# Seven-product output projection: weight sums formed by GpSimd in attention steps 9 to 12, token-tile differences stored by the stages that make the tiles

## The chip, the cores and the metric

The kernel runs on one core of one Trainium2 chip. Five engines work side by side and meet only at semaphores: PE (TensorE, the matmuls), VectorE (DVE), ScalarE (ACT), GpSimd (POOL) and SyncE (SP), which here only issues DMAs. Each engine takes its instructions in program order, so an instruction that waits holds everything behind it on its engine. The metric is the device time of one execution in microseconds; the profile gives the span from the first to the last instruction of one execution.

## What is computed

One decoder layer with two parallel groups of heads, in float32. Cut to what matters:

```python
h    = rms_norm(x, pre_norm_w) * (1 + scale) + shift       # x: 2048 tokens x 1024
proj = h @ w_in                                            # GLA and SSD columns
o    = gla_chunked(q, k, v, log_a)                         # 4 heads, 1024 columns
o    = rms_norm(o, gla_norm_w) * silu(g)
y    = ssd_chunked(xs, dt, A, B, C) + d_skip * xs          # 2 groups, 1024 columns
y    = rms_norm(y * silu(z), ssd_norm_w)
mixed = concat(o, y) @ w_out                               # 2048 x 2048 @ 2048 x 1024
out  = x + gate * rms_norm(mixed, post_norm_w)
```

## The kernel before

Every large product is taken in three passes: a float32 value is split into a high part (ScalarE copies it to the rounded format) and a low part (VectorE subtracts the high part from the raw value), and PE adds high*high, high*low and low*high.

**front** (`front`) makes h and runs the GLA heads. It has 16 steps, `n`, four blocks of 512 tokens for each of four heads. A step has twelve slots `i` of some 3.5 us; in each PE does half a projection unit (`half_unit`) and one small piece of the attention of the step before: `scores` (L1066, L1069), `outputs` (L1079 to L1085) or `turn` (L1093), for tiles t = 0 to 3. For each tile ScalarE takes the mean square (L574), GpSimd turns it into 1/rms (`rstd_of`, L419 and L422), ScalarE scales (L578), PE transposes (L1093) and VectorE multiplies with the gate (`gated`, L808) into `y`. At slot 11 VectorE also makes the exponentials' products (`products`, L776 to L782), which PE needs in the first slot of the next step. SyncE's queue holds in each step the four loads of h for the step after the next (`load_h`, L302; each waits until VectorE has read the buffer, L737), in steps 3, 7, 11 and 15 also the six weight loads of the next head (`load_w`, L283; each waits for the `w_low`, L748, of two units before), and at the end `store_y` (L312), two DMAs that put `y` into the DRAM tensor `y_d` ("mixed_in"). The tile `late` (3 x 1024 columns) serves steps 5 to 7 and the end; between, it is free.

**ssd** (`ssd`) has 2 groups of 8 steps of 256 tokens. In a step PE does eight projection units (L1727, L1731) with the pieces of the step before between them. In the last step of all (15) SyncE loads the output weights of the first product (`load_w` with g = G, L1307): both halves of 512 columns, 512 KB each time, and VectorE subtracts one from the other (`w_minus`, L1572) before ScalarE and VectorE split the result (L1441, L1567). The first two units of the output projection run at the end of this stage (L1744).

**project_out** (`project_out`) multiplies 2048 x 2048 by 2048 x 1024 by Strassen's scheme: the tokens are taken as pairs of 128-token tiles, the columns in two halves, and `PRODUCTS` lists seven products, each of a sum of tiles and a sum of weight blocks. A unit `j` is one product for one pair of tiles (eight pairs, 56 units, 24 matmuls of 512 columns each, L2124). For unit `j` SyncE loads the tiles (`load_a`, L1918, L1920, L1923), GpSimd adds or subtracts them where the product has two terms (`a_sum`, L1980 to L1983), ScalarE takes the high part (`a_high`, L2022) and VectorE the low part (`a_low`, L2067), three units ahead on GpSimd and two on the others. Likewise for each of the 48 weight pieces of products 1 to 6: `load_w`, `w_sum` (32 of them), `w_high` (L2032), `w_low` (L2073). VectorE adds the results (`add`, L2087). A finished row of 128 tokens goes through ScalarE (`square`, L2046), GpSimd (`rstd_of`, L2000, L2003) and VectorE (`finish`, L2096, L2100) and is stored. During product 6 (j = 48 to 55) a row is finished per unit.

The order is written out by hand in the loops over `j`: on ScalarE a_high(j+2), w_high, copy(j), square; on VectorE a_low(j+2), the row of the unit before (`finish`), w_low, add(j); on GpSimd a_sum(j+3), w_sum, rstd.

```python
for j in range(IN_TAIL, N + 1):          # VectorE
    if j + 2 < N:
        a_low(j + 2)
    for m in range(len(rows)):
        if square_at[m] + 1 == j:
            finish(m)
```

## Time and profile before

| | us |
|---|---|
| three runs | 1753.59, 1759.62, 1761.76; median 1759.62 |
| the profiled execution | 1755.11, its span 1753.3 |
| PE busy | 1641.5 (94%) |
| VectorE busy | 1025.4 (58%) |
| ScalarE busy | 843.3 (48%) |
| GpSimd busy | 401.0 (23%) |
| front, by the last PE work before the gap | about 0 to 792 |
| ssd | about 797 to 1416 |
| project_out | 1421.1 to 1753.3 |

PE's figure is time in which a matmul was open, not its peak. Its granted clock has two levels, 1.0 (2.4 GHz) and 0.5 (1.2 GHz), and was 0.975 in the mean of the span. The page's strip of 40 slices shows PE at eight or nine tenths from the third slice to the last but one, and VectorE rising from four tenths in front over seven in ssd to nine at the end. So a time is read from PE's gaps: where they are, what ended them, and at what clock PE worked after them.

### The profile page before, as it was taken

The page shows a single profiled execution, that of the slowest core. Times are in us where ns is not written, and L with a number is a line of the kernel's source. Part 1 is how long each engine was busy: PE and PEld are TensorE (multiplying, and loading weights), DVE is VectorE, ACT ScalarE, POOL GpSimd, SP SyncE. Part 2 cuts the span into 40 slices and gives each one's busy share as a digit, 9 for nine tenths or more (in the row PEclk, how much of TensorE's full clock was granted, in tenths as well). Part 3 has the DMA queues.
Part 4 walks back from the last instruction along what each step waited for, and adds up shares of the span by engine and source line. Part 5 has one row for each costly group of instructions (what it writes and reads, how often), then busy time and mean ns, then how long its engine had stood idle before and what let it go on. Part 6 is the DMA issues. An engine that isn't in the chain of part 4 may idle for free. (4 is left out here: it accounts for less than half of the span.)

```text
span 1753.3 us, 27317 instructions
## 1 busy us (share of the span) xinstructions
PE 1641.5 (94%) x10022; PEld 1409.5 (80%) x10022; DVE 1025.4 (58%) x1744; ACT 843.3 (48%) x1496; POOL 401.0 (23%) x441
## 2 busy tenths in 40 slices
PE   5799899999999999988999998999999889999985
PEld 5688788887888888878888887888888768888864
DVE  4443444453444443355677767777766746866986
ACT  5555455545544554464445555544554533334222
POOL 5000000010000001000222221222222237762652
PEclk9999999999999999998999999999999899999997
DMA  9422152235212421224212125212223357876785
GB/s 285 147 91 98 49 170 71 67 109 166 63 61 70 135 73 61 84 61 132 67 64 68 67 91 161 86 67 67 72 79 100 109 197 262 290 260 229 295 291 167
DMA packets 126622, 222.75 MB, mean 127 GB/s; under 512 B 9267, under 2 KB 77123, under 8 KB 122422
## 3 DMA queue, kind: packets, MB, share of 16 engines
q1 hardware_dynamic: 121302, 203.34, 36.0%
q10 hardware_dynamic: 4384, 17.83, 2.8%
q0 software_dynamic: 832, 0.22, 0.2%
q8 instruction: 62, 1.02, 0.2%
q14 instruction: 42, 0.34, 0.1%
HBM read 187.54 MB, written 33.82 MB: 126 GB/s over the span
## 5 line engine op out<-in xcount | busy, mean ns | idle before, releaser
L1042 PE MATMUL ps<-hl,w 128*128 128x512 f32 x1488 | 374.7, 401 | 0.1
L1042 PEld LDWEIGHTS ps<-hl,w 128*128 128x128 f32 x1488 | 275.8, 189 | 57.2 <-issue 1.4
L1727 PE MATMUL ps<-hl,w 128*128 128x256 f32 x2304 | 295.7, 289 | 4.7 <-PEq L266 4.7
L1727 PEld LDWEIGHTS ps<-hl,w 128*128 128x128 f32 x2304 | 283.6, 194 | 13.1 <-issue 13.1
L1048 PE MATMUL ps<-w,hl 128*128 128x256 f32 x1536 | 204.6, 291 | 2.0 <-DVE w L748 2.0
L1048 PEld LDWEIGHTS ps<-w,hl 128*128 128x128 f32 x1536 | 194.6, 195 | 4.9 <-DVE w L748 2.4
L2124 PE MATMUL ps<-w,hl 128*128 128x512 f32 x720 | 173.6, 403 | 14.0 <-DVE hl L2067 5.3
L1731 PE MATMUL ps<-hl 128*128 128x512 f32 x768 | 178.6, 391 | 0.0
L1600 DVE SCALAR_TENSOR_TENSOR c_acc<-c_before,conv_col,c_acc 128x256 f32<-128x256 f32 x288 | 142.0, 493 | 62.1 <-ACT c_acc L1462 55.1
L2124 PEld LDWEIGHTS ps<-w,hl 128*128 128x128 f32 x720 | 139.9, 196 | 47.1 <-DVE hl L2067 7.5
L1731 PEld LDWEIGHTS ps<-hl 128*128 128x128 f32 x768 | 143.0, 188 | 29.3
L419 POOL TENSOR_SCALAR mse<-ms 128x1 f32<-128x1 f32 x60 | 15.8, 263 | 636.6 <-ACT squares L574 636.6
L1460 ACT ACTIVATE c_before<-ps 128x256 f32<-128x256 f32 x96 | 36.9, 384 | 216.0 <-PE ps L1727 216.0
L2124 PE MATMUL ps<-hl 128*128 128x512 f32 x576 | 131.8, 390 | 2.6 <-DVE hl L2067 2.6
L2124 PEld LDWEIGHTS ps<-hl 128*128 128x128 f32 x576 | 108.0, 188 | 25.9 <-DVE hl L2067 3.5
L798 DVE SCALAR_TENSOR_TENSOR state<-state,dec,ps 128x256 f32<-128x256 f32 x56 | 26.9, 480 | 134.7 <-PE ps L1085 134.7
L737 DVE TENSOR_TENSOR hl<-x_sb,hl 128x1024 fp32r<-128x1024 f32 x48 | 58.7, 1222 | 57.5 <-ACT hl L558 57.5
L1399 POOL TENSOR_TENSOR c_yi<-c_yi,c_xd 128x512 f32<-128x512 f32 x32 | 41.3, 1291 | 186.5 <-DVE c_yi L1640 186.5
L1384 POOL TENSOR_TENSOR c_xend<-c_xdt,tok 128x512 f32<-128x512 f32 x32 | 33.5, 1046 | 215.6 <-DVE c_xdt L1620 215.6
L2067 DVE TENSOR_TENSOR hl<-d_a_raw,hl 128x1024 fp32r<-128x1024 f32 x35 | 63.6, 1818 | 25.7 <-ACT hl L2022 25.6
L748 DVE TENSOR_TENSOR w<-w_raw,w 128x1024 fp32r<-128x1024 f32 x30 | 36.5, 1223 | 59.3 <-ACT w L504 59.3
L808 DVE SCALAR_TENSOR_TENSOR y<-ps,norm_col,gz 128x128 f32<-128x128 f32 x120 | 36.3, 344 | 55.2 <-PE ps L1093 43.2
(251 smaller groups left out, 2648.5 us busy)
## 6 DMA issues: line engine op xcount, KB each, us to landing
x_sb<-h SPq DMA_DIRECT2D x52, 512.0 KB, 3.9
d_a_raw<-mixed_in SPq DMA_DIRECT2D x22, 1024.0 KB, 7.2
w_raw<-in_w_in SPq DMA_DIRECT2D x42, 512.0 KB, 4.5
c_ac<-step_sums ACTq DMA_DIRECT2D x16, 1024.0 KB, 4.7
w_raw<-in_w_out SPq DMA_DIRECT2D x32, 512.0 KB, 4.9
c_h_raw<-h SPq DMA_DIRECT2D x56, 256.0 KB, 2.8
late_w<-mixed_in SPq DMA_DIRECT2D x10, 1024.0 KB, 7.3
d_a_raw<-mixed_in SPq DMA_DIRECT2D x18, 512.0 KB, 4.7
```

What stands on the lines that cost most here:

```text
L737: last = dve.tensor_tensor(hl[:, n % 2, ks, LO, :], raw, hl[:, n % 2, ks, HI, :].bitcast(F32), ALU.subtract)
L748: dve.tensor_tensor(lo, w_raw[:, u % 2], hi.bitcast(F32), ALU.subtract).then_inc(w_ready, 1)
L808: last = dve.scalar_tensor_tensor(out=y[:, t, f, :], in0=ps[:, TURNS, f * P:(f + 1) * P], scalar=norm_col[:, f:f + 1], in1=gz[:, r % 2, f, ...
L1042: mm = pe.matmul(ps[:, PROJ + u % 2, :], w[:, u, k, a, :], hl[:, par, k, b, :], start=(k == 0 and i == 0), stop=(k == KT - 1 and i == 2))
L1048: mm = pe.matmul(ps[:, PROJ + u % 2, half * DV:(half + 1) * DV], hl[:, par, k, a, t * P:(t + 1) * P], w_v[:, k, b, :], start=(k == 0 and i ...
L1399: pool.tensor_tensor(yi[:, :, :], yi[:, :, :], xd[:, :, :], ALU.add).then_inc(skip_ready, 1)
L1460: act.activation(before[:, u, HIST:], ps[:, PROJ + u % 2, 0:B2], ACT.Copy)
L1600: op = dve.scalar_tensor_tensor(out=acc[:, u, :], in0=before[:, u, k:k + B2], scalar=conv_col[:, k, ch:ch + 1], in1=acc[:, u, :], op0=ALU. ...
L1727: mm = pe.matmul(ps[:, PROJ + u % 2, 0:B2], w[:, u, k, a, :], hl[:, par, k, b, :], start=(k == 0 and i == 0), stop=(k == KT - 1 and i == 2))
L1731: mm = pe.matmul(ps[:, PROJ + u % 2, :], hl[:, par, k, a, t * P:(t + 1) * P], w_z[:, k, b, :], start=(k == 0 and i == 0), stop=(k == KT - ...
L2067: dve.tensor_tensor(half[:, :, LO, :], a_term(j, 0).rearrange("p (f n) -> p f n", n=P), half[:, :, HI, :].bitcast(F32), ALU.subtract).then ...
L2124: mm = pe.matmul(ps[:, j % 8, :], halves[:, j % 4, k, a, :], weight(i)[:, k, b, :], start=(k == 0 and q == 0), stop=(k == KT - 1 and q == 2))
```

## The change

It does four things.

1. **Sums of weights in front.** In steps 9 to 12 SyncE loads, for each of the eight row blocks f of `w_out`, the four 128 x 512 quarters (1 MB, `load_quarters`) into `late`, GpSimd makes five sums (`out_sum`: 4 = 1-3, 5 = 0+1, 1 = 0+3, 3 = 2+3, 2 = 2-0) and SyncE stores the five (1280 KB, `store_sums`) into the DRAM tensor `w_sum_d`. Two blocks are done in a step. The next block is loaded only when the stores of the block before have landed (`small_stored`).
2. **Differences of tiles.** After each step of front VectorE makes `y_diff`, tile 1 minus tile 0 of each pair (128 x 512), and SyncE stores it as a third tile of `y_d`; in ssd GpSimd does it (`c_y_diff`, 128 x 512). `y`'s buffer is free again when all three stores have landed.
3. **ssd's last step** loads the ready difference of the weights (256 KB) and drops `w_minus`.
4. **project_out** loads every weight piece as one piece of 256 KB; `w_sum` is gone (32 instructions). Products 1 and 6 take the stored tile difference as one term: 16 of the 40 `a_sum` are gone, 24 are left. Products, rows and order are otherwise as they were.

Besides, `squares` is written in bfloat16 and some small tiles share memory.

```diff
@@ front, SyncE
                 def put_y(n):
                     h, s = n // NB, n % NB
                     for b in range(B1 // B2):
-                        sp.dma_start(y_d[s * (B1 // B2) + b, :, :, h * 2:h * 2 + 2, :],
+                        sp.dma_start(y_d[s * (B1 // B2) + b, :, 0:2, h * 2:h * 2 + 2, :],
                                      y[:, 2 * b:2 * b + 2, :, :]).then_inc(y_stored, 16)
+                    sp.wait_ge(diff_ready, n + 1)
+                    sp.dma_start(y_d[s * (B1 // B2):(s + 1) * (B1 // B2), :, 2, h * 2:h * 2 + 2, :]
+                                 .rearrange("b p f n -> p b f n"), y_diff[:, :, :, :]).then_inc(y_stored, 16)
+
+                def load_quarters(f):
+                    sp.wait_ge(small_stored, 32 + f * 16)
+                    sp.dma_start(quarters[:, 0:4, :].rearrange("p (s c) n -> p s (c n)", s=2), out_rows[f]
+                                 ).then_inc(rows_loaded, 16)
+
+                def store_sums(f):
+                    sp.wait_ge(out_summed, 5 * f + 5)
+                    sp.dma_start(w_sum_d[f], quarters[:, 1:6, :]).then_inc(small_stored, 16)
...
                     for q in range(KT // 2):
+                        if q == 2 and SUMS_AT <= n < SUMS_AT + KT // 2:
+                            store_sums(2 * (n - SUMS_AT))
+                            load_quarters(2 * (n - SUMS_AT) + 1)
                         if NB <= n + 2 <= STEPS:
                             load_h(n + 2, q)
...
                     if n > 0:
                         store_y(n - 1)
+                    if SUMS_AT <= n < SUMS_AT + KT // 2:
+                        store_sums(2 * (n - SUMS_AT) + 1)
+                    if SUMS_AT - 1 <= n < SUMS_AT + KT // 2 - 1:
+                        load_quarters(2 * (n - SUMS_AT) + 2)
@@ front, GpSimd
+                def out_sum(f, i):
+                    if i == 0:
+                        pool.wait_ge(rows_loaded, 32 + 16 * f + 16)
+                    to, a, b, op = ((4, 1, 3, ALU.subtract), (5, 0, 1, ALU.add), (1, 0, 3, ALU.add), (3, 2, 3, ALU.add),
+                                    (2, 2, 0, ALU.subtract))[i]
...
+                    pool.tensor_tensor(quarters[:, to, :], quarters[:, a, :], quarters[:, b, :], op).then_inc(out_summed, 1)
...
                 for n in range(STEPS):
                     if n > 0:
                         rstd_of((n - 1) * TB)
+                    if SUMS_AT <= n < SUMS_AT + KT // 2:
+                        for i in range(3):
+                            out_sum(2 * (n - SUMS_AT), i)
...
                     if n > 0:
                         for t in range(1, TB):
                             rstd_of((n - 1) * TB + t)
+                            if SUMS_AT <= n < SUMS_AT + KT // 2:
+                                for i in ((3, 4), (0, 1, 2), (3, 4))[t - 1]:
+                                    out_sum(2 * (n - SUMS_AT) + t // 2, i)
@@ front, VectorE
                     last.then_inc(y_ready, 1)
+                    if t == TB - 1:
+                        difference(r * TB + TB)
+
+                def difference(done):
+                    dve.wait_ge(y_ready, done)
+                    dve.tensor_tensor(y_diff[:, :, :, :], y[:, 1::2], y[:, 0::2], ALU.subtract).then_inc(diff_ready, 1)
@@ ssd, SyncE (store_y), GpSimd, VectorE
+                    sp.wait_ge(diff_ready, r + 1)
+                    sp.dma_start(y_d[bass.ds(b, 1), :, TB2, f:f + XT, :].rearrange("a p f n -> (a p) f n"),
+                                 y_diff[:, :, :]).then_inc(y_stored, 16)
...
                     for t in range(TB2):
                         rstd_of(r, t)
+                    pool.wait_ge(y_ready, r * TB2 + TB2)
+                    wait(pool, y_stored, r * 32)
+                    pool.tensor_tensor(y_diff[:, :, :], y[:, 0], y[:, 1], ALU.subtract).then_inc(diff_ready, 1)
...
-                        if last_of_group and g + 1 == G and u > 0:
-                            if u > 1:
-                                w_low(G, u - 2)
-                            w_minus(u - 1)
@@ project_out
-    (((0, 0, -1), (1, 0, 1)), ((0, 0, 1), (0, 1, 1)), (((1, 1), 1),)),
+    (((2, 0, 1),), ((0, 0, 1), (0, 1, 1)), (((1, 1), 1),)),
...
-    (((0, 1, 1), (1, 1, -1)), ((1, 0, 1), (1, 1, 1)), (((0, 0), 1),)),
+    (((2, 1, 1),), ((1, 0, 1), (1, 1, 1)), (((0, 0), 1),)),
 )
+W_SUMS = (3, 4, 0, None, 1, None, 2)
...
-                    for v in W_AT.get(j, ()):
-                        w_sum(v)
```

**SyncE's queue around step 11 of front.** The first listing is of before, the second of the change; L numbers are each file's own, a row is one kind of instruction with its count. `w_raw<-in_w_in` is a weight load, `x_sb<-h` a load of h, `w_sums<-late` a `store_sums`, `late<-in_w_out` a `load_quarters`.

```order
58 L283 DMA w_raw<-in_w_in 128x8x128 x2
59 L302 DMA x_sb<-h 128x1024
60 L283 DMA w_raw<-in_w_in 128x8x128
61 L302 DMA x_sb<-h 128x1024
62 L283 DMA w_raw<-in_w_in 128x8x128 x2
63 L302 DMA x_sb<-h 128x1024
64 L283 DMA w_raw<-in_w_in 128x8x128
```

```order
77 L330 DMA w_sums<-late 128x2560
78 L325 DMA late<-in_w_out 128x2x1024
79 L288 DMA w_raw<-in_w_in 128x8x128 x2
80 L307 DMA x_sb<-h 128x1024
81 L288 DMA w_raw<-in_w_in 128x8x128
82 L307 DMA x_sb<-h 128x1024
83 L288 DMA w_raw<-in_w_in 128x8x128 x2
84 L330 DMA w_sums<-late 128x2560
85 L325 DMA late<-in_w_out 128x2x1024
86 L307 DMA x_sb<-h 128x1024
87 L288 DMA w_raw<-in_w_in 128x8x128
```

One store and one load of sums stand ahead of the head's first weight load, and another pair stands in the middle of the step, behind the fourth and fifth weight loads.

**GpSimd in steps 9 to 12.** Before, it holds only the pairs `mse`, `rstd`, one for each tile; here are two and a half such pairs, and then the change in step 9.

```order
101 L419 TENSOR_SCALAR mse<-ms 128x1
102 L422 TENSOR_TENSOR rstd<-mse,neg_half 128x1
103 L419 TENSOR_SCALAR mse<-ms 128x1
104 L422 TENSOR_TENSOR rstd<-mse,neg_half 128x1
105 L419 TENSOR_SCALAR mse<-ms 128x1
```

```order
106 L445 TENSOR_TENSOR rstd<-mse,neg_half 128x1
107 L456 TENSOR_TENSOR late<-late 128x512 x3
108 L442 TENSOR_SCALAR mse<-ms 128x1
109 L445 TENSOR_TENSOR rstd<-mse,neg_half 128x1
110 L456 TENSOR_TENSOR late<-late 128x512 x2
111 L442 TENSOR_SCALAR mse<-ms 128x1
112 L445 TENSOR_TENSOR rstd<-mse,neg_half 128x1
113 L456 TENSOR_TENSOR late<-late 128x512 x3
114 L442 TENSOR_SCALAR mse<-ms 128x1
115 L445 TENSOR_TENSOR rstd<-mse,neg_half 128x1
116 L456 TENSOR_TENSOR late<-late 128x512 x2
```

Three sums now stand between the 1/rms of tiles 0 and 1 and between those of tiles 2 and 3, two behind those of tiles 1 and 3.

**VectorE in ssd's last step.** `c_acc` is the convolution, `w_raw<-w_raw` is `w_minus`, `c_yi` begins `tile_out`.

```order
1104 L1600 SCALAR_TENSOR_TENSOR c_acc<-c_before,conv_col,c_acc 128x256 x3
1105 L1572 TENSOR_TENSOR w_raw<-w_raw 128x512
1106 L1600 SCALAR_TENSOR_TENSOR c_acc<-c_before,conv_col,c_acc 128x256 x3
1107 L1580 TENSOR_TENSOR hl<-c_h_raw,hl 128x4x128
1108 L1567 TENSOR_TENSOR w<-w_raw,w 128x512
1109 L1572 TENSOR_TENSOR w_raw<-w_raw 128x512
1110 L1640 TENSOR_TENSOR c_yi<-ps,tok 128x512
```

```order
1120 L1647 SCALAR_TENSOR_TENSOR c_acc<-c_before,conv_col,c_acc 128x256 x6
1121 L1619 TENSOR_TENSOR w<-w_raw,w 128x512
1122 L1627 TENSOR_TENSOR hl<-c_h_raw,hl 128x4x128
1123 L1687 TENSOR_TENSOR c_yi<-ps,tok 128x512
```

Both `w_minus` ahead of `c_yi` are gone, and the one split that is left stands behind the second convolution.

## Rows read from the trace of the kernel before

**Rows 1.** Waits of PE: who, for what, us in total, times, longest.

```profile
PE ps L2124 <- DVE hl L2067: 7.9, 5, 2.9
...
PE ps L1772 <- DVE c_btok L1629: 7.3, 3, 3.7
...
PE ps L1066 <- DVE y L808: 9.7, 7, 2.3
...
PE ps L1066 <- DVE dec L782: 4.5, 10, 0.5
```

**Rows 2.** Stretches of L2124: us, PE busy (matmuls), clock, DMA share, GB/s.

```profile
1421.10:1657.20 236.10, 235.49 (x1026) 0.99 0.79 272
...
1657.20:1737.70 80.50, 69.09 (x271) 0.92 0.75 249
```

**Rows 3.** PE in order of time: start, us, line [idle before <-releaser].

```profile
1456.07 43.74 PE L2124 MATMUL ps<-hl 128*128 128x512 f32 x192
```

**Rows 4.** All engines after an idle stretch: the clock is third from the end.

```profile
1421.00:1425.00 4.00, 3.86 (x9) 3.12 (x10) 0.00 (x0) 1.08 (x2) 0.13 (x2) 0.50 0.68 181
```

**Rows 5.** VectorE in order of time, inside the last product.

```profile
1693.32 0.68 DVE L2087 TENSOR_TENSOR d_mixed<-d_mixed,ps 128x512 f32<-128x512 f32 x1
...
1696.16 3.41 DVE L2067 TENSOR_TENSOR hl<-d_a_raw,hl 128x1024 fp32r<-128x1024 f32 x1 [2.17 <-ACT hl L2022]
...
1701.95 0.68 DVE L2087 TENSOR_TENSOR d_mixed<-d_mixed,ps 128x512 f32<-128x512 f32 x1
...
1730.65 1.23 DVE L2067 TENSOR_TENSOR hl<-d_a_raw,hl 128x1024 fp32r<-128x1024 f32 x1 [2.17 <-ACT hl L2022]
...
1744.88 0.68 DVE L2087 TENSOR_TENSOR d_mixed<-d_mixed,ps 128x512 f32<-128x512 f32 x1
```

**Rows 6.** GpSimd in order of time, same row of output.

```profile
1696.11 2.39 POOL L1982 TENSOR_TENSOR d_a_raw<-d_a_raw 128x1024 f32<-128x1024 f32 x1
```

**Rows 7.** PE in order of time, SSD steps 15 and 8.

```profile
1107.01 1.15 PE L1772 MATMUL ps<-c_xdt,c_decay 128*64 128x64 f32 x32
...
1108.66 6.31 PE L1727 MATMUL ps<-hl,w 128*128 128x256 f32 x48
...
1368.37 1.97 PE L1772 MATMUL ps<-c_xdt,c_decay 128*64 128x64 f32 x32 [3.32 <-DVE c_btok L1629]
...
1371.36 7.80 PE L1727 MATMUL ps<-hl,w 128*128 128x256 f32 x48
```

**Rows 8.** VectorE in order of time, SSD step 15.

```profile
1358.30 0.69 DVE L1572 TENSOR_TENSOR w_raw<-w_raw 128x512 f32<-128x512 f32 x1 [4.07 <-DMA w_raw<-in_w_out]
...
1368.03 0.28 DVE L1629 COPY c_btok<-ps 128x128 f32<-128x128 f32 x1
```

**Rows 9.** SyncE's queue in order of time, end of step 10 and step 11.

```profile
570.05 1.20 SPq L312 DMA_DIRECT2D mixed_in<-y  x2
...
591.52 11.06 SPq L283 DMA_DIRECT2D w_raw<-in_w_in  x2
```

**Rows 10.** DMA issues: out<-in, engine, count, KB each, median us to landing.

```profile
c_ac<-step_sums ACTq DMA_DIRECT2D x16, 1024.0 KB, 4.7
...
mixed_in<-c_y SPq DMA_DIRECT2D x16, 512.0 KB, 3.0
```

**Rows 11.** One microsecond of a store: DMA share and GB/s stand last.

```profile
1015.00:1016.00 1.00, 1.00 (x11) 1.00 (x10) 0.93 (x3) 0.00 (x0) 0.00 (x0) 1.00 1.03 403
```

**Rows 12.** GpSimd's addition of two 128x512 tiles: busy, mean ns, idle before.

```profile
L1399 POOL TENSOR_TENSOR c_yi<-c_yi,c_xd 128x512 f32<-128x512 f32 x32 | 41.3, 1291 | 186.5 <-DVE c_yi L1640 186.5
```

**Rows 13.** PE in order of time, step 11: second and last transposition.

```profile
587.10 0.38 PE L1093 MATMUL ps<-ident,o_n 128*128 128x128 f32 x2
...
608.39 0.38 PE L1093 MATMUL ps<-ident,o_n 128*128 128x128 f32 x2
```

**Rows 14.** VectorE in order of time, end of step 11.

```profile
608.21 1.23 DVE L737 TENSOR_TENSOR hl<-x_sb,hl 128x1024 fp32r<-128x1024 f32 x1 [2.01 <-ACT hl L558]
```

**Rows 15.** ScalarE in order of time, SSD step 7.

```profile
1056.03 1.06 ACT L1437 ACTIVATE w<-w_raw 128x1024 fp32r<-128x1024 f32 x1 [4.71 <-DMA w_raw<-in_w_in]
```

136 lines of the change are left out of this document (60 added, 76 removed).

## The prediction

> **What bounds the kernel now.** I read the list of waits first, then each engine in order of time at the places that the change touches, then the DMA issues. PE is open 94% of the span, so only its gaps and the clock behind them can be won or lost. The list of PE's waits shows 7.9 us in the projection for VectorE's low parts, 7.3 us in ssd for `c_btok` (3.7 the longest), 9.7 us in front for `y`, and ten very short waits for the exponentials' products (`dec`, at most 0.5 us) [rows 1]. Those ten cost nothing, but they say that VectorE has no room at the end of a step of front. The table by stretch shows the projection's matmuls back to back at clock 0.99 up to 1657.2; from there to 1737.7, where PE ends, 271 of them took 80.50 us [rows 2]. Undisturbed, 192 take 43.74 us, so 0.228 each and 5.47 for a unit of 24 [rows 3]. The 271 would be 61.8 us: 18.7 us are lost in the last product and the end of the one before it, in gaps and in matmuls at half clock behind them. A gap costs more than itself: the four microseconds from 1421, right behind the empty stretch between ssd and the projection, ran at 0.50 [rows 4], and the 9 matmuls in them are 2.1 us at full clock. So I put 1.9 to 2.8 us on top of a gap of several us and nothing on one under 1 us.
>
> The sum is made against the profiled execution, 1755.11 us, which lies 4.5 us (0.3%) under the median of the three runs, 1759.62. I forecast the difference and take it from the median.
>
> **Gain 1, the projection's last product.** Why it is slow stands on VectorE. `a_low` takes 3.41 us at 1696.16 and 1.23 us at 1730.65, same shape and form [rows 5]. The difference is GpSimd: its `a_sum` began at 1696.11 and held 2.39 us [rows 6]; the last unit has none beside it. So the two exclude each other, and the later one waits 2.18. From addition to addition, VectorE's round for a unit is 1701.95 - 1693.32 = 8.6 us [rows 5] against PE's 5.47: VectorE is the bound. The changed kernel takes the stored difference in product 6, so no `a_sum` stands beside these eight units: 8.6 - 2.2 = 6.45 a round. This is still over 5.47; VectorE stays the bound, only less. Undisturbed PE would end at 1657.2 + 61.8 = 1719, and unit 48, seven units earlier, at 1681. From there five rounds of 6.45 and two of some 5.3 (the last have no `a_low`) end near 1724, where the last addition was at 1744.88 [rows 5]: 21 us, and at most 22. VectorE comes out of product 5 behind, though, since `a_sum` remains there and its rounds have little to spare beside PE's. I take **19.5**, range 14 to 22.
>
> The Trainium skill, page "SBUF — State Buffer", section "Who interferes with whom", says: VectorE and GpSimd share a pair of ports under an exclusive lock, a VectorE instruction with two SBUF inputs needs it, and whoever starts first holds it for the whole instruction. By that rule the trace agrees, 3.41 against 1.23; it also speaks against the front half of this change (cost 3).
>
> **Gain 2, ssd's step 15.** VectorE waits 4.07 us there for 512 KB of `w_out` and then subtracts; `c_btok`, behind it in order, comes at 1368.03 [rows 8], and PE stood 3.32 us for it, from 1365.05 [rows 7]. The unit behind this stop took 7.80 us where the same unit in step 8 took 6.31; from the start of the L1772 matmuls to that unit's end it is 10.79 us in step 15 and 7.96 in step 8 [rows 7], so 2.8 are the clock. With both `w_minus` and this wait gone (4.07 + 0.69 for the one shown) `c_btok` comes before PE asks. 3.3 + 2.8, nearly: **6**, range 2 to 7 (another load behind it may be late next).
>
> **Cost 1, the second pair in step 11.** SyncE's queue is in order, and step 11 loads the next head's weights, each when a `w_low` has freed its buffer. Two were issued in the 11.06 us from 591.52, the second at 602.6 [rows 9]. The change puts `store_sums` and `load_quarters` of the odd block behind them. Store issued at about 602.4; 3.0 us for the first 512 KB [rows 10] and 1.95 for the other 768 KB at 403 GB/s [rows 11], with some queueing 5.2 (up to 6). Then the load of 1 MB, 4.7 by the row of the same size [rows 10], 4.9 beside other traffic, and the two weight loads in front of it some 1.2 more. The quarters are there at about 613.8. GpSimd holds three sums ahead of the 1/rms of tile 3: 3 x 1.29 by its addition of the same size [rows 12] = 3.9; the two small instructions of the 1/rms 0.9 and ScalarE's scaling 0.5, both my estimates: 619.1. PE transposes tile 3 at 608.39 today [rows 13]. Stall **10.7** (9 to 14), and **2.5** of half clock behind it [rows 4]. Nothing covers it: everything on PE stands behind this transposition.
>
> **Cost 2, the first pair at step boundaries.** Let T0 be 21.0 us ahead of tile 1's transposition, 566.1 for the one at 587.10 [rows 13]; it is the step's start on PE. `store_y` is issued at 570.05 [rows 9], T0 + 3.9. Behind it now come VectorE's difference and its store, then `store_sums` at T0 + 5.7, with the `y` transfers still in flight: landed T0 + 11.7, quarters T0 + 16.7, three sums to T0 + 20.6, 1/rms and scaling to T0 + 22.0. So 1.0 in each of steps 10 and 11, **2.0** together (0 with a quick round trip; 6 with half clock). Steps 9 and 12 have slack: in 9 the load is issued a step early, 12 begins behind the stall. The odd blocks of steps 9, 10 and 12 meet no weight load: sums by T0 + 39, the 1/rms of tile 3 at T0 + 39.7; no stall, with 0.7 to spare.
>
> **Cost 3, sums beside VectorE at the end of a step.** The last two sums of a step stand behind the 1/rms of tile 3, and VectorE then takes the low part of h, two SBUF inputs, 1.23 at 608.21 [rows 14], and behind it the products for which PE waits already [rows 1]. One sum ahead of it delays it by up to 1.29 [rows 12]. Three boundaries (steps 9, 10, 12; in 11 it drowns in the stall) x 1.2 = **3.6**, range 0 to 4. By the skill's rule it is nothing where VectorE starts first; the sum would then be 3.6 lower.
>
> **Small ones.** The difference of 128x512 (0.69, as `w_minus` [rows 8]) stands ahead of low parts that PE waits for in steps 1 and 2, and the third store delays `y`'s release once: **2.3** (0 to 4). In the other steps it hides in the time in which `y` waits for ScalarE and GpSimd. At the ends of front and ssd a difference and a 256 KB store (under the 3.0 of 512 KB [rows 10]) stand behind the last `y`, partly beside the stores of before: **1.3** (0 to 4). In ssd's step 7 the weight load waits behind `diff_ready` on SyncE, and ScalarE already waits 4.71 for it [rows 15], PE 3.7 behind that [rows 1]: **1.5** (0 to 3). GpSimd's other differences in ssd lie in its idle time, 186 us before one line alone [rows 12]. `w_sum` gone from the projection gives nothing up to 1657, since nothing is lost there [rows 2].
>
> **Sum.** Gains 19.5 + 6 = 25.5. Costs 10.7 + 2.5 + 2.0 + 3.6 + 2.3 + 1.3 + 1.5 = 23.9. Net -1.6: 1753.5 on the profile's scale, **1758.0** on the median's. A measurement of this kernel tells about 0.5% from no change, 8.8 us: 1750.8 to 1768.4 is the same.
>
> **Rivals.**
> (A) *The round trip is quick.* Store and load take 8 us instead of 10.1, VectorE starts first at the boundaries, and the projection gains its full 22. For it: doubling a transfer from 512 KB to 1 MB added only 1.7 us [rows 10]. Cost 1 falls by 2.1, cost 2 by 2.0, cost 3 by 3.6, gain 1 rises by 2.2, the small ones fall by 1: -1.6 - 10.9 = -12.5, so 1747.
> (B) *Slower: the round trip takes 13 us.* Its place is the wait for the landed stores ahead of every `load_quarters`. For it: the store is larger than any in the trace, and loads of h and `y` share the queue. Tile 1 in steps 10 and 11 then stalls 4.1 instead of 1.0 (+6.2, and +5 of half clock), step 11's second pair costs 3.1 more, the odd blocks of 9, 10 and 12 some 0.8 each: +16.8, so -1.6 + 16.8 = +15.2: 1775. It decides from about 12 us on. Against it: 4.7 for 1 MB [rows 10].
> (C) *The projection gains 10 only*, because VectorE leaves product 5 more than a unit behind, with up to 2.4 of exclusion for each `a_sum` [rows 6]: +9.5, 1767.5. Against it: up to 1657.2 PE lost nothing [rows 2].
>
> The same skill's page "DMA: Bandwidth & Descriptors", section "Anatomy of one DMA — SWDGE (gpsimd) path", puts about 2 us fixed on each transfer of GpSimd's queue. These transfers are SyncE's, and no run here shows whether it carries over; by it store and load would be 5.0 + 4.4 = 9.4 us, cost 1 0.7 lower.
>
> **Chances.** My forecast 0.42, (A) 0.30, (B) 0.19, (C) 0.09, half of which falls to either side of the bound. Faster by over 0.5%: 0.30; within: 0.46; slower: 0.24. The range, 1743 to 1776, takes in most of (A) and (B); what lies outside is a round trip under 7 or over 13 us.
>
> **What would show it.** Right: one gap of some 11 us in step 11 ahead of the last transposition, released by ScalarE behind GpSimd's sums behind the quarters; `a_low` at 1.23 throughout product 6 and its round at 6.45; no gap at `c_btok` in step 15, a longer one in step 7. Wrong: gaps of more than 2 us at tile 1 in steps 10 and 11, or at tile 3 in steps 9, 10, 12 (B); an `a_low` of 3 us in product 6, or additions late at its start (C); a store and load well under 10 us from issue to landing (A). The forecast fails altogether if the loss in the last 100 us has another cause than VectorE's round: then PE's gaps there stay.

## The result

| | before | changed | ratio |
|---|---|---|---|
| median of 11 runs, us | 1757.92 | 1771.04 | 1.0064, 95% interval 1.0048 to 1.0081 |
| lowest and highest, us | 1753.59, 1764.65 | 1766.75, 1775.01 | |
| span of the profiled execution, us | 1753.3 | 1767.4 | |

The changed kernel is slower, by 0.64%, some 11 to 14 us. The forecast was 1.6 us faster. The two spans differ by 14.1 us, and it can be split at the two places where PE waits for its sequencer, the starts of ssd (796.72 before, 838.84 after) and of the projection (1421.14 and 1457.70):

| stage | before, us | changed, us | difference | forecast |
|---|---|---|---|---|
| front | 796.7 | 838.8 | +42.1 | +21.6 |
| ssd | 624.4 | 618.9 | -5.6 | -3.7 |
| projection | 332.2 | 309.7 | -22.5 | -19.5 |
| sum | 1753.3 | 1767.4 | +14.1 | -1.6 |

The forecast column shares the prediction's 1.3 us for the ends of the stages out as 0.5 for front and 0.8 for ssd. So two stages came out as forecast or better, and front cost twice what it was to cost.

The waits of PE in the changed kernel (who, for what; us in total, times, longest) answer to [rows 1]. The projection's wait for `hl` is gone; a new wait of 24 us for `o_n`, ScalarE's scaled tile, stands first:

```profile
PE ps L1140 <- ACT o_n L618: 24.0, 8, 11.9
```

**The projection.** Two stretches of PE's matmuls there, as in [rows 2]: us, PE busy (matmuls), clock, DMA share, GB/s. There is no gap left; the 8.6 us rounds of [rows 5] are 1728.93 - 1722.49 = 6.44 us, and `a_low` takes 1.23 throughout:

```profile
1457.70:1710.00 252.30, 252.29 (x1103) 0.99 0.69 232
1710.00:1754.10 44.10, 44.07 (x195) 1.00 0.67 209
```

```profile
1718.89 1.23 DVE L2086 TENSOR_TENSOR hl<-d_a_raw,hl 128x1024 fp32r<-128x1024 f32 x1 [2.17 <-ACT hl L2044]
...
1722.49 0.68 DVE L2106 TENSOR_TENSOR d_mixed<-d_mixed,ps 128x512 f32<-128x512 f32 x1
...
1728.93 0.68 DVE L2106 TENSOR_TENSOR d_mixed<-d_mixed,ps 128x512 f32<-128x512 f32 x1
```

**Front, tile by tile.** The changed kernel's transposition of a tile, less the same one before, is 6.9 us at the start of step 9 and 41.7 us at the start of step 13; it is 41.8 in step 15 too. All of the loss beyond the first 6.9 us lies in the four steps that form sums. PE in order of time there (start, us, line, count, [idle before <- who ended it]), the counterparts of [rows 13]: the last transpositions of steps 9, 10 and 11, the second of step 11, and the first matmul of step 11:

```profile
534.12 0.64 PE L1140 MATMUL ps<-ident,o_n 128*128 128x128 f32 x2 [2.90 <-ACT o_n L618]
...
581.15 0.44 PE L1140 MATMUL ps<-ident,o_n 128*128 128x128 f32 x2 [1.71 <-ACT o_n L618]
...
586.82 0.33 PE L1113 MATMUL ps<-ident,k_end 128*128 128x128 f32 x1 [2.47 <-DVE dec L822]
...
606.95 0.44 PE L1140 MATMUL ps<-ident,o_n 128*128 128x128 f32 x2 [2.42 <-ACT o_n L618]
...
641.89 0.69 PE L1140 MATMUL ps<-ident,o_n 128*128 128x128 f32 x2 [11.93 <-ACT o_n L618]
```

The forecast had the 11.93 us (as 10.7) and stops at tile 1 of steps 10 and 11 (1.0 each; 1.08 and 2.42 came). It had nothing at tile 3 of steps 9, 10 and 12 (2.90, 1.71 and 1.91) and nothing at tile 1 of step 12 (1.80).

What GpSimd does at these places: it waits for the quarters (`late<-in_w_out`), forms three sums, and only then makes the 1/rms that ScalarE and PE wait for:

```profile
528.72 3.89 POOL L456 TENSOR_TENSOR late<-late 128x512 f32<-128x512 f32 x3 [9.75 <-DMA late<-in_w_out]
532.69 0.22 POOL L442 TENSOR_SCALAR mse<-ms 128x1 f32<-128x1 f32 x1
...
636.54 3.82 POOL L456 TENSOR_TENSOR late<-late 128x512 f32<-128x512 f32 x3 [19.47 <-DMA late<-in_w_out]
```

And SyncE's queue: `store_sums`, then `load_quarters`, which waits for the landing of the store, so the distance between the two issues is the store's time. The rows at the end of step 10 and in step 11 answer to [rows 9]:

```profile
515.30 0.43 SPq L330 DMA_DIRECT2D w_sums<-late  x1
523.73 0.38 SPq L325 DMA_DIRECT2D late<-in_w_out  x1
...
541.77 0.50 SPq L330 DMA_DIRECT2D w_sums<-late  x1
547.77 0.38 SPq L325 DMA_DIRECT2D late<-in_w_out  x1
...
614.22 9.76 SPq L288 DMA_DIRECT2D w_raw<-in_w_in  x2
624.03 0.58 SPq L330 DMA_DIRECT2D w_sums<-late  x1
631.02 0.37 SPq L325 DMA_DIRECT2D late<-in_w_out  x1
```

The store of 1280 KB took 8.4 us right behind a load of h (515.30 to 523.73), 6.0 behind `y` (541.77 to 547.77) and 7.0 behind two weight loads (624.03 to 631.02); the load then took 5.0 (528.72 - 523.73), 5.1 and 5.5. Over all seven pairs the store took 7.3 to 8.4 us where a load of h stands right in front, 6.0 to 6.8 behind `y`, and store and load together took 10.9 to 13.4 us. The forecast put 10.1 for the two alone, 11.0 behind `y` (cost 2) and 11.4 behind the weight loads (cost 1); rival (B) put 13.

### The profile page after: what moved, and what is told of

Its sections match the earlier page's. It is cut to its first block and busy times, and to the rows that moved or that the text cites. A ratio compares the mean times of both kernels' runs of the same rounds, so it can differ in the third digit from the quotient of the medians.

```text
span 1767.4 us, 27409 instructions
## 1 busy us (share of the span) xinstructions
PE 1637.2 (93%) x10022; PEld 1407.8 (80%) x10022; DVE 1044.2 (59%) x1752; ACT 842.1 (48%) x1496; POOL 387.2 (22%) x449
## 5 line engine op out<-in xcount | busy, mean ns | idle before, releaser
L1089 PE MATMUL ps<-hl,w 128*128 128x512 f32 x1488 | 380.4, 405 | 0.1
L1647 DVE SCALAR_TENSOR_TENSOR c_acc<-c_before,conv_col,c_acc 128x256 f32<-128x256 f32 x288 | 161.9, 563 | 47.0 <-ACT c_acc L1514 40.1
L2143 PE MATMUL ps<-w,hl 128*128 128x512 f32 x720 | 166.3, 393 | 5.1 <-PEq L1347 5.1
L2143 PEld LDWEIGHTS ps<-hl 128*128 128x128 f32 x576 | 108.1, 188 | 22.5
L777 DVE TENSOR_TENSOR hl<-x_sb,hl 128x1024 fp32r<-128x1024 f32 x48 | 63.2, 1317 | 80.8 <-ACT hl L598 80.8
L618 ACT ACTIVATE o_n<-ps,rstd 128x256 f32<-128x256 f32 x60 | 28.5, 475 | 96.6 <-POOL rstd L445 96.6
L456 POOL TENSOR_TENSOR late<-late 128x512 f32<-128x512 f32 x40 | 54.0, 1360 | 73.8 <-DMA late<-in_w_out 72.6
```

Source lines behind the costliest of these rows:

```text
L456: pool.tensor_tensor(quarters[:, to, :], quarters[:, a, :], quarters[:, b, :], op).then_inc(out_summed, 1)
L777: last = dve.tensor_tensor(hl[:, n % 2, ks, LO, :], raw, hl[:, n % 2, ks, HI, :].bitcast(F32), ALU.subtract)
L1089: mm = pe.matmul(ps[:, PROJ + u % 2, :], w[:, u, k, a, :], hl[:, par, k, b, :], start=(k == 0 and i == 0), stop=(k == KT - 1 and i == 2))
L1647: op = dve.scalar_tensor_tensor(out=acc[:, u, :], in0=before[:, u, k:k + B2], scalar=conv_col[:, k, ch:ch + 1], in1=acc[:, u, :], op0=ALU. ...
L2143: mm = pe.matmul(ps[:, j % 8, :], halves[:, j % 4, k, a, :], weight(i)[:, k, b, :], start=(k == 0 and q == 0), stop=(k == KT - 1 and q == 2))
```

## The experiments

All ratios are against the kernel before, run on the same chip. "Distance" is the start of a PE transposition in the profile of a kernel less the start of the same one in the kernel before.

### What the sums cost in all

```diff
@@ e1_no_sums, from the changed kernel
-                            store_sums(...); load_quarters(...)      # all of them
-                                    out_sum(...)                     # all of them
-                        src = w_sum_d[f, :, W_SUMS[i], :]
+                        src = w_rows[f, :, 0, 0:HN]
```

> The changed kernel without the loads, sums and stores of w_out in front; ssd and the projection read plain quarters of w_out in the places of the sums, with the same bytes and instructions (so the product is another one). Theory 1 (the 35 us that front loses in steps 9 to 12 all hang on the sums): 1771 - 35 = 1736 us, ratio to before 0.988. Theory 2 (a good part of it is the tile differences on VectorE and SyncE): 1745 to 1755. The 6.9 us lost before step 9 stay under both.

Measured: 1732.3 us, ratio 0.9868 (0.9847 to 0.9889). The steps 9 to 12 of front lose nothing (the distance to before is 1.7 us at the start of step 9 and 1.8 in step 15), ssd is 618.5 and the projection 309.9 us long as in the changed kernel. So the sums cost 35 us in steps 9 to 12; theory 1. The other 4 to 5 us of the difference lie ahead of step 9, where this profile has lost 1.7 us and not the 6.9 that both theories had left in place.

### Is it step 11, the length of the round trip, or the sums themselves?

```diff
@@ e2_skip11, from the changed kernel: SyncE and GpSimd
+    SUM_STEPS = (9, 10, 12, 13)
-                        if q == 2 and SUMS_AT <= n < SUMS_AT + KT // 2:
+                        if q == 2 and n in SUM_STEPS:
```

> The sums in steps 9, 10, 12 and 13; step 11, which loads the next head's weights, has none. All eight blocks are made, nothing else is moved. Theory 1a (step 11's 12 us stall is the weight loads on SyncE's queue in front of the odd block's store): step 11 costs nothing, step 13 costs what step 12 does (4 to 6 us): 18 - 5 = 13 us less, 1758. Theory R (the sums themselves, which shut VectorE out of its ports, cost the time wherever they are): 1768 to 1771.

Measured: 1753.7 us, ratio 0.9979 (0.9963 to 0.9995), 17.3 us under the changed kernel. In step 11 nothing is lost. Tile 3 of steps 9, 10 and 12 and tile 1 of step 10 keep their stops, and step 13 has stops of its own. The two rows are tile 3 of steps 9 and 12:

```profile
532.59 0.53 PE L1141 MATMUL ps<-ident,o_n 128*128 128x128 f32 x2 [2.73 <-ACT o_n L619]
...
667.95 0.44 PE L1141 MATMUL ps<-ident,o_n 128*128 128x128 f32 x2 [2.27 <-ACT o_n L619]
```

In the changed kernel steps 11 and 12 grow by 18.4 and 6.1 us; here steps 12 and 13, with the same four blocks, grow by 4.5 and 6.5. So theory 1a is shown: the weight loads in front of the store are worth 13 to 14 us of the 35. The other 21 are in the steps with sums wherever these stand.

```diff
@@ e4_short_store, from the changed kernel
-                    sp.dma_start(w_sum_d[f], quarters[:, 1:6, :]).then_inc(small_stored, 16)
+                    sp.dma_start(w_sum_d[f, :, 0:1], quarters[:, 1:2, :]).then_inc(small_stored, 16)
```

> The changed kernel, but of the five sums of a block only one is stored (256 KB instead of 1280 KB) and every reader reads that one; loads, sums and their order stay. Theory 1 (length of the round trip): the store takes 3 to 3.5 us instead of 6 to 8, so the round trip 8.5 instead of 12.5; the stalls at tile 3 in steps 9, 10 and 12 and at tile 1 in steps 10, 11 and 12 go, that of step 11's tile 3 falls from 11.9 to 8: 14 to 16 us less, 1756. Theory R: 1770, nothing changes.

Measured: 1751.8 us, ratio 0.9966 (0.9944 to 0.9987), 19 us less. With 256 KB the store takes 2.9 us behind `y` (536.35 to 539.28), and 4.7 behind a load of h:

```profile
513.24 0.43 SPq L330 DMA_DIRECT2D w_sums<-late  x1
517.95 0.38 SPq L325 DMA_DIRECT2D late<-in_w_out  x1
...
536.35 0.51 SPq L330 DMA_DIRECT2D w_sums<-late  x1
539.28 0.38 SPq L325 DMA_DIRECT2D late<-in_w_out  x1
```

The stops at tile 1 and at tile 3 of steps 9 and 10 are gone and that of tile 3 of step 12 is 0.3 us; 9.4 us are left in step 11 (11.9 with the long store). All 40 sums are still there. What this run leaves standing is a second, smaller thing that the long stops had covered: at the steps' boundaries PE waits 2.2 us (2.5 at the last) for `dec` instead of 0.4. Two things make up these 1.8 us. GpSimd's last two sums run from 528.08 to 530.74, and VectorE's low part of h, 1.23 us in [rows 14], takes 2.22 beside the second of them: 1.0. It also starts 0.8 us later against PE's transposition than in the kernel before, because ScalarE makes the high part of h behind the scaling of tile 3, and that stands behind the late 1/rms:

```profile
528.08 2.66 POOL L456 TENSOR_TENSOR late<-late 128x512 f32<-128x512 f32 x2
```

```profile
529.60 2.22 DVE L777 TENSOR_TENSOR hl<-x_sb,hl 128x1024 fp32r<-128x1024 f32 x1 [2.77 <-ACT hl L598]
```

```profile
534.36 0.33 PE L1113 MATMUL ps<-ident,k_end 128*128 128x128 f32 x1 [2.20 <-DVE dec L822]
```

By the rule of the Trainium skill weighed in the prediction (page "SBUF — State Buffer", section "Who interferes with whom") this would be nothing if VectorE starts first. It did not: GpSimd started 1.5 us earlier and its second sum, begun at about 529.4, was under way when VectorE started at 529.60, so the trace agrees with the rule, and here it is GpSimd that starts first.

### The same sums where their quarters have landed

```diff
@@ e3_spread, from e2_skip11: GpSimd and SyncE
                         rstd_of((n - 1) * TB)
+                    if n in SUM_STEPS:
+                        for i in range(5):
+                            out_sum(2 * SUM_STEPS.index(n), i)
...
                             rstd_of((n - 1) * TB + t)
+                            if n in SUM_STEPS and t == 2:
+                                for i in range(5):
+                                    out_sum(2 * SUM_STEPS.index(n) + 1, i)
...
+                        if q == 1 and n in SUM_STEPS:
+                            store_sums(2 * SUM_STEPS.index(n))
+                            load_quarters(2 * SUM_STEPS.index(n) + 1)
+                        if q == 3 and n in SUM_STEPS:
+                            store_sums(2 * SUM_STEPS.index(n) + 1)
+                            load_quarters(2 * SUM_STEPS.index(n) + 2)      # but the last
```

> As the run before, and each block's five sums stand together where its quarters have landed already: behind the 1/rms of tile 0 and of tile 2; its store and the next load stand on SyncE between the loads of h. Theory 1 (PE stalls because GpSimd holds the 1/rms behind sums that wait for a round trip of 12 to 13 us): no stall above 1 us is left in steps 9 to 13, front loses the 7 us before step 9 and 1 to 3 more: 1771 - 33 = 1738, ratio 0.989. Theory R (port exclusion of the 40 sums, 54 us on GpSimd): at least half of the 35 us stays, over 1752.

Measured: 1730.2 us, ratio 0.9852 (0.9835 to 0.9868): 41 us under the changed kernel, 28 under the one before, with the same 40 sums, the same eight stores and loads and the same bytes. The distance to the kernel before is 4.0 us at the start of step 9 and 4.1 at the start of step 14, behind the last step with sums. GpSimd's five sums are 7.62 us in one piece and start without a wait, at once behind the 1/rms of tile 0; the work for tile 1 is due 9.4 us after their start:

```profile
494.74 0.22 POOL L445 TENSOR_SCALAR mse<-ms 128x1 f32<-128x1 f32 x1 [9.65 <-ACT squares L617]
...
495.58 7.62 POOL L459 TENSOR_TENSOR late<-late 128x512 f32<-128x512 f32 x5
505.01 0.22 POOL L445 TENSOR_SCALAR mse<-ms 128x1 f32<-128x1 f32 x1 [1.82 <-ACT squares L617]
```

```profile
503.22 0.34 SPq L331 DMA_DIRECT2D w_sums<-late  x1
507.91 0.38 SPq L326 DMA_DIRECT2D late<-in_w_out  x1
...
523.72 0.33 SPq L331 DMA_DIRECT2D w_sums<-late  x1
529.98 0.38 SPq L326 DMA_DIRECT2D late<-in_w_out  x1
```

The store takes 4.7 us where it is issued 2.5 us behind a load of h (503.22 to 507.91) and 6.3 where it is issued 1.2 us behind one (523.72 to 529.98). Theory 1 is shown; the exclusion between the 40 sums and VectorE costs PE nothing in steps 9, 10, 12 and 13, where VectorE has slack. The time is 8 us under the expected 1738, since the steps with sums lose nothing and the first eight lost 4.0 us in this profile, not 7.

```diff
@@ e5_spread_with_11, from e3_spread
-    SUM_STEPS = (9, 10, 12, 13)
+    SUM_STEPS = (9, 10, 11, 12)
```

> e3_spread, but with the sums in steps 9, 10, 11 and 12 as in the changed kernel: only the order on GpSimd and SyncE differs from it. Theory 1 (GpSimd's order decides): in step 11 the second block's store waits for the weight loads, its load lands some 12 us into step 12, and the sums of that step, which stand behind the 1/rms of tile 0, end before tile 1 needs its own: at most 2 us are lost, 1730 to 1733. Rival 1a (the weight loads on SyncE's queue cost by themselves, whatever the order): 8 to 12 us of step 11's stall are back, 1740 or more.

Measured: 1737.5 us, ratio 0.9886 (0.9863 to 0.9909). In the profile the steps 9 to 12 lose 3.6 us, between the two theories and near the first. They stand at three places: ahead of tile 3's `outputs` in step 11, at the first slot of step 12, and ahead of tile 1's `outputs` in step 12:

```profile
613.28 0.28 DVE L831 COPY_PREDICATED att<-causal,ps 128x128 f32<-128x128 int32 x1
613.67 0.67 PE L1129 MATMUL ps<-v,att 128*128 128x256 f32 x2 [0.95 <-issue]
...
622.93 0.33 PE L1116 MATMUL ps<-ident,k_end 128*128 128x128 f32 x1 [1.51 <-DVE dec L825]
...
635.05 0.61 DVE L851 SCALAR_TENSOR_TENSOR y<-ps,norm_col,gz 128x128 f32<-128x128 f32 x2 [3.74 <-DMA mixed_in<-y_diff]
...
637.86 0.67 PE L1129 MATMUL ps<-v,att 128*128 128x256 f32 x2 [1.28 <-issue]
```

The profile names nothing for the first and the last ("issue"), but `outputs` waits for `att`, and VectorE's copy of `att` ends just before PE goes on (613.28 + 0.28, and 637.47 + 0.29). It is late in step 11 because the low part of h ahead of it takes 1.80 us beside the five sums, and in step 12 because VectorE first waits 3.74 us for the store of `y_diff`, which now lies behind a store and a load of sums in the queue, and then takes 1.97 us for the low part of h beside the next sums. The 1.51 us come from the 1/rms of tile 3: it stands behind five sums that took 9.40 us here, and ScalarE's high part of h stands behind it. So in this order too the sums cost something around the step in which VectorE also splits the next head's weights.

The rest of the 7 us to e3_spread lies ahead of step 9, where the two kernels are the same. So it was run again:

> e5_spread_with_11 once more. Its profile was 4.9 us later than e3_spread at the start of step 9 although the two are the same up to there. Scatter of one execution: this time the first eight steps lie 1 to 5 us behind the kernel before and the time is 1733 to 1738. A property of the program: 8 to 9 us again.

Measured: 1737.1 us, ratio 0.9863 (0.9840 to 0.9886), and 5.6 us at the start of step 9 instead of 8.9; steps 9 to 12 lose 4.1. So the 8.9 was scatter in part: the distance is 0.6 above the expected 1 to 5, and the time is in the expected range. Here the copy of `att` in step 11 is later still: PE stops 1.85 us for it at 611.24, and the four microseconds from 611 have a granted clock of 0.60. Of the 7 us to e3_spread's median some 4 are these two steps; why the other 3 stay is open.

### Where the projection's gain comes from

```diff
@@ e7_before_no_a6, from the kernel before: PRODUCTS, product 6
-    (((0, 1, 1), (1, 1, -1)), ((1, 0, 1), (1, 1, 1)), (((0, 0), 1),)),
+    (((0, 1, 1),), ((1, 0, 1), (1, 1, 1)), (((0, 0), 1),)),
```

> The kernel before with one term less in product 6: its tiles are loaded and taken alone, so the eight a_sum of the last product are left out (the result of that product is another one). Theory D: rounds of 6.45 instead of 8.6, 1758 - 18 = 1740, ratio 0.990. Theory W: w_sum is still there and VectorE comes late out of product 5: gain of 10 at most, 1748.

Measured: 1741.0 us, ratio 0.9910 (0.9886 to 0.9933), 17 us less. That is theory D. The projection is 316.8 us long, 15.4 less than before; `a_low` is 1.8 us in the first two units of product 6 and 1.2 in the other six, and the round from addition to addition is 1699.62 - 1693.18 = 6.44:

```profile
1696.03 1.22 DVE L2067 TENSOR_TENSOR hl<-d_a_raw,hl 128x1024 fp32r<-128x1024 f32 x1 [2.17 <-ACT hl L2022]
```

```diff
@@ e6_sums_only, from e3_spread: no y_diff anywhere, PRODUCTS 1 and 6 as before
-    (((2, 1, 1),), ((1, 0, 1), (1, 1, 1)), (((0, 0), 1),)),
+    (((0, 1, 1), (1, 1, -1)), ((1, 0, 1), (1, 1, 1)), (((0, 0), 1),)),
```

> e3_spread without any difference of tiles: products 1 and 6 form theirs by a_sum on GpSimd as the kernel before does, all else as in e3_spread. Theory D (the projection's gain is product 6 without a_sum): 21 us of the gain are lost and 4 us of front and 1 of ssd come back: 1730 + 16 = 1746. Theory W (the 32 w_sum that are gone carry half of the projection's gain): 1735.

Measured: 1738.6 us, ratio 0.9903 (0.9871 to 0.9936), between the two theories. Its projection is 326.1 us long, 6.1 less than before, without any difference of tiles: the missing `w_sum`, with weight loads of half the size, are worth that; the two were not taken apart. 15.4 + 6.1 = 21.5 is nearly the 22.5 of both together. In product 6 its VectorE stands as in [rows 5], and PE's waits for `hl` are back, 2.82 us the longest:

```profile
1680.38 3.41 DVE L2073 TENSOR_TENSOR hl<-d_a_raw,hl 128x1024 fp32r<-128x1024 f32 x1 [2.17 <-ACT hl L2031]
```

This run also prices the differences in ssd: its ssd is 615.1 us long, 9.3 less than before, where e3_spread has 618.7. So `w_minus` and its wait were worth 9.3, and the stored differences cost 3.6 of it.

### Are the differences worth their price?

```diff
@@ e8_ssd_diffs, from e3_spread: front makes and stores no difference
-    (((2, 0, 1),), ((0, 0, 1), (0, 1, 1)), (((1, 1), 1),)),
+    (((0, 0, -1), (1, 0, 1)), ((0, 0, 1), (0, 1, 1)), (((1, 1), 1),)),
```

> e3_spread without the differences in front: they serve product 1 alone, where PE loses nothing; product 1 goes back to a_sum, product 6 keeps the differences that ssd makes. Theory F (front's differences cost 2 to 5 us of late y and give nothing): 1726 to 1728, ratio 0.983. Rival (product 1's a_sum shuts VectorE out and PE waits there, or the 4 us are scatter of the first steps): 1730 to 1736.

Measured: 1727.0 us, ratio 0.9826 (0.9807 to 0.9846). The projection is as long as in e3_spread (308.8 and 308.6), so product 1's differences gave nothing. Run again:

> e8_ssd_diffs once more, beside the run before on the same chip: 1727; its first eight steps of front within 2 us of the first time.

Measured: 1728.2, ratio 0.9823 (0.9807 to 0.9838). The distance to before at the start of step 9 is 1.5 and 0.3 us in these two, -0.2 in e6_sums_only, 2.7 and 1.4 in the two runs below: 1.1 in the mean of the five. In the seven profiles whose front makes differences ahead of step 9 (the changed kernel, e1 to e5 and e5_again) it is 6.9, 1.7, 5.5, 4.0, 4.8, 8.9 and 5.6, in the mean 5.3. So they cost some 4 us. Most of it stands in step 7: from its first to its last transposition all seven lose 3.0 to 4.7 us, and the five without differences between -0.7 and 2.3. In the changed kernel VectorE waits 8.74 us for the third store before it can write `y` (5.66 us for the stores of `y` in the kernel before), and PE stops 4.05 us behind it (0.97 before):

```profile
413.02 0.61 DVE L848 SCALAR_TENSOR_TENSOR y<-ps,norm_col,gz 128x128 f32<-128x128 f32 x2 [8.74 <-DMA mixed_in<-y_diff]
```

The intervals of e3_spread and e8_ssd_diffs overlap; that the difference of 2 to 3 us is real rests on these anchors, not on the times.

```diff
@@ e9_diff_later, from e8_ssd_diffs: GpSimd in ssd
-                    for t in range(TB2):
-                        rstd_of(r, t)
-                    pool.wait_ge(y_ready, r * TB2 + TB2)
-                    wait(pool, y_stored, r * 32)
-                    pool.tensor_tensor(y_diff[:, :, :], y[:, 0], y[:, 1], ALU.subtract).then_inc(diff_ready, 1)
+                    rstd_of(r, 0)
+                    if not (isinstance(r, int) and r == 0):
+                        difference(r - 1)      # waits for y_stored >= r * 32 + 16 of its own r
+                    rstd_of(r, 1)
```

> e8_ssd_diffs with GpSimd's difference of ssd moved: it stands between the 1/rms of the two tiles of the next step, where GpSimd is idle, and its store one step later on SyncE. Theory P (the 3.9 us that the differences cost in ssd come from VectorE being shut out: its three convolution instructions take 3.02 us beside GpSimd's difference and 1.53 without): ssd 615 to 616 us long instead of 619, 1724 in all. Rival S (they come from the second store on SyncE and its wait): 1727, ssd unchanged.

What it rests on: VectorE's three convolution instructions (`c_acc` x3) in step 8 of ssd, in e8_ssd_diffs, what GpSimd does there, and then the same three in e6_sums_only:

```profile
1096.73 3.02 DVE L1640 SCALAR_TENSOR_TENSOR c_acc<-c_before,conv_col,c_acc 128x256 f32<-128x256 f32 x3 [1.47 <-ACT c_acc L1507]
```

```profile
1095.46 1.30 POOL L1463 TENSOR_TENSOR c_y_diff<-c_y 128x512 f32<-128x512 f32 x1 [10.46 <-ACT c_y L1548]
1096.72 1.05 POOL L1427 TENSOR_TENSOR c_xend<-c_xdt,tok 128x512 f32<-128x512 f32 x1
1097.72 1.24 POOL L1434 TENSOR_TENSOR c_decayed<-c_state,c_chunk 128x512 f32<-128x512 f32 x1
```

```profile
1093.93 1.53 DVE L1634 SCALAR_TENSOR_TENSOR c_acc<-c_before,conv_col,c_acc 128x256 f32<-128x256 f32 x3 [1.46 <-ACT c_acc L1501]
```

The expectation reads this as exclusion by the difference itself. The rows say it otherwise: the difference ended when the convolution began. It had pushed back the two GpSimd instructions behind it, and these now lie beside the convolution; in e6_sums_only they are over at 1092.8, before the convolution starts.

Measured: 1727.1 us, ratio 0.9813 (0.9797 to 0.9828): no less than e8_again's 1728.2 beyond what can be told apart. ssd is 619.3 us long, where theory P had 615 to 616, so by its numbers this is rival S; the trace shows that theory P's stops did go and another came. The stops at `c_btok` in step 8 (0.95 in e8_again) and step 15's tail (1.71) fell to nothing and 0.94, but the gap between the stages grew from 5.11 to 7.81 us, because the last difference now stood behind the landing of the last `y`; without these 2.7 us ssd would be 616.6:

```profile
1414.61 1.26 POOL L1477 TENSOR_TENSOR c_y_diff<-c_y 128x512 f32<-128x512 f32 x1 [6.62 <-DMA mixed_in<-c_y]
```

```profile
1418.36 6.94 PE L2152 MATMUL ps<-w,hl 128*128 128x512 f32 x22 [7.81 <-PEq L1340]
```

```diff
@@ e10_tail_diff, from e9_diff_later: the last difference alone
-                    pool.wait_ge(y_stored, r * 32 + 16)
+                    pool.wait_ge(y_stored, r * 32 + (0 if last else 16))
```

> e9_diff_later, in which the last difference of ssd waited for the landing of the last y (GpSimd idle 6.6 us before it). Here it waits for the store of the difference before alone, so it is made while y is stored. Theory P: PE's gap between ssd and the projection falls from 7.8 to 5.1 us, ssd is 616 to 617 us long, the whole 1724 to 1725, ratio 0.980. Rival S (PE waits for the stores either way): no change, 1727.

Measured: 1726.2 us, ratio 0.9810 (0.9786 to 0.9834). The gap is 5.07 us again and ssd 617.2 us long, 0.8 to 1.8 less than in the two runs of e8, which is theory P. It is still 2.1 more than in e6_sums_only; what these are was not tried. The time is the lowest of all, by less than the runs can tell:

```profile
1413.38 11.95 PE L2153 MATMUL ps<-w,hl 128*128 128x512 f32 x43 [5.07 <-PEq L1340]
```

So there are versions that compute the whole layer and are faster than both kernels: e3_spread by 1.5%, e8_ssd_diffs by 1.8% and e10_tail_diff by 1.9% against the kernel before.

## Why the prediction was wrong

Its steps one by one, in us, with what the traces and runs show (e1 to e10 are the experiments). The six costs from cost 1 to the differences in front add up to the 41.7 us of front:

| step | forecast | measured | from |
|---|---|---|---|
| gain 1, projection | 19.5 | 22.5 | stage lengths; 15.4 by product 6 (e7), 6.1 by `w_sum` (e6) |
| gain 2, step 15 | 6 | 9.3 over all of ssd | e6 against before |
| cost 1, second pair of step 11 | 13.2 | 14.2 | distance from tile 2 of step 11 to tile 0 of step 12; 11.93 is the gap |
| between tiles 1 and 2 of step 11 | 0 | 1.6 | distance; a stop of 1.30 us for `att`, as in e5 |
| cost 2, tile 1 of 10, 11, 12 | 2.0 | 5.8 | distance of transpositions: 1.3, 2.6, 2.0 |
| tile 3 of 9, 10, 12 | 0 | 7.0 | distance: 3.1, 1.9, 2.1; all but gone in e4 |
| cost 3, boundaries 10, 11, 13 | 3.6 | 6.2 | distance: 3.0 of longer waits for `dec`, the rest half clock; 1.8 to 2.1 each without half clock, in e4 |
| differences in front, up to step 9 | 2.3 | 6.9 (mean 5.3 of seven) | distance at step 9 |
| differences in ssd | 2.3 | 3.6 | e3 against e6 |

**The step that failed** is in cost 2: the places in steps 9, 10 and 12 that it priced at nothing, by the sentences "The odd blocks of steps 9, 10 and 12 meet no weight load: sums by T0 + 39 ... no stall, with 0.7 to spare" and "Steps 9 and 12 have slack: ... 12 begins behind the stall". PE stopped at tile 3 in all three steps and at tile 1 of step 12 as well; these four cost 9.0 us without the half clock behind them. The load was right (4.9 forecast; 4.9 to 5.5). Behind `y` the store was right too: cost 2 put 6.0 us for it, it took 6.0 in step 10, and the stop there was 1.08 for 1.0. But the odd blocks' store is handed out right behind a load of h, where the prediction had no row for such a pair; its price of a store was 5.2, the store took 7.3 to 8.4, and with its load 12.5 to 13.4 us. A slack of 0.7 us, worked out from estimates, was treated as a place without cost and not as a coin toss. That the length of the store decides is shown by e4_short_store, where the store takes 4.7 at the same place and the stops at tile 3 are gone or 0.3 us, and e3_spread shows that nothing but the placing of sums, stores and loads is at fault.

This was rival (B)'s mechanism: (B)'s text has the reason, "loads of h and `y` share the queue", and its 1775 was nearer than the forecast; it was given 0.19. Its sum was nearer partly by luck. It put 11.2 us more than the forecast on tile 1 of steps 10 and 11, where 1.9 came, and 2.4 on the odd blocks, where 7.0 came.

**The second part that failed** is what a stop costs besides itself. The prediction put half clock only on the 11 us stop. The clock of the four microseconds behind the stops of 2.90, 2.42, 11.93 and 1.91 us (all engines; the clock is third from the end):

```profile
534.00:538.00 4.00, 3.88 (x11) 3.17 (x12) 2.95 (x3) 1.50 (x3) 2.08 (x2) 0.57 0.01 2
607.00:611.00 4.00, 4.00 (x20) 3.33 (x21) 3.97 (x6) 2.55 (x4) 2.09 (x2) 1.00 0.46 124
642.00:646.00 4.00, 4.00 (x11) 3.23 (x12) 3.19 (x3) 1.27 (x2) 1.85 (x2) 0.50 0.00 0
690.00:694.00 4.00, 4.00 (x14) 3.06 (x13) 3.21 (x3) 1.24 (x2) 1.83 (x2) 0.66 0.02 2
```

0.57, 1.00, 0.50 and 0.66: the stops of 2.90 and 1.91 us were followed by matmuls at the lower of the two levels (1.2 GHz) for most of the stretch, that of 2.42 was not, nor were those of 1.71, 1.80 and 2.47. So the length of the stop alone does not decide it; what does stays open. From the first, the distance grew by 2.1 us up to the next transposition, 0.4 of it a longer wait for `dec`: the stop of 2.9 cost some 1.7 more, and in the same way that of 1.91 some 1.5. "Nothing on one under 1 us" held.

**Cost 3** had half of the mechanism. In e4_short_store VectorE is late by 1.8 us a boundary, not 1.2: 1.0 is the second of GpSimd's last sums beside the low part of h, and 0.8 is the late 1/rms of tile 3, behind which ScalarE makes the high part. In the changed kernel the longer waits for `dec` are 3.0 us over the three boundaries, under the 3.6 forecast; the other 3.2 there are half clock. The boundary behind the stall in step 11 has no wait for `dec` of its own, as forecast.

**Gain 1** had the right size for another reason than it gave. Of the 22.5 us, product 6's `a_sum` is 15.4 (forecast 19.5 with 14 as the lower end), and the missing `w_sum` bring 6.1, on which the prediction said "gives nothing up to 1657, since nothing is lost there". That is true up to 1657 to within some 2 us, but behind it lies the end of product 5, which belonged to the stretch that the prediction had counted as lost and given to `a_sum` alone. VectorE's round there, in the kernel before: `a_low`, the first half of `finish` and `w_low`, which take 1.2, 1.3 and 0.7 us undisturbed:

```profile
1661.14 2.76 DVE L2067 TENSOR_TENSOR hl<-d_a_raw,hl 128x1024 fp32r<-128x1024 f32 x1
1663.83 2.31 DVE L2096 SCALAR_TENSOR_TENSOR d_mixed<-d_mixed,d_rstd,d_gate_row 128x1024 f32<-128x1024 f32 x1
...
1667.32 2.88 DVE L2073 TENSOR_TENSOR w<-w_raw,w 128x512 fp32r<-128x512 f32 x1
```

All three are long beside `a_sum` and `w_sum`; at the same unit of e6_sums_only, without `w_sum`, only the last is (2.90 us), and of the changed kernel none. Rival (C), which had VectorE come late out of product 5, named the place; it came late, and the dropped `w_sum` took most of this away too.

**Gain 2** was right in direction and 3 us short: the unit of step 15 is as fast as in the other steps, and later waits of the stage for `c_z` fell as well (2.50 before, 1.46 after). **Step 7** of ssd, forecast to lose 1.5 on the weight loads, lost nothing: its stop at `c_btok` is 3.74 in both kernels; the cost of ssd's differences is in step 8 and at the end, where GpSimd's next two instructions, pushed back by the difference, lie beside VectorE's convolution (e8, e9).

The other rivals: (A), the quick round trip, was wrong throughout in the changed kernel, though its 8 us nearly appear in e4_short_store (2.9 and 5). The range, 1743 to 1776, held the time, at its upper end; the direction was not the one forecast.

## What to carry to other kernels

Where an engine with instructions in order is given background work between urgent ones, place the work where its data has long been there, and the urgent one behind it has slack for the whole of it: the same 40 sums, stores and loads cost 35 us in one order, 4 in another in the same four steps, and nothing once the step with the weight loads was left out too. A slack that comes out of a sum of estimates and is smaller than their error is an even chance of a stop, and it should be priced at each place where it occurs, with half-clock time behind some of the stops. A transfer's time is to be read from a row with the same neighbours in the queue, not from the same size alone.
